# Opening by channel halves, the gate input mixed one stage later, and the middle stage's small vector work moved

## The reference

```
mod = silu(c) @ ada_w[0] + ada_b[0]            # shift sh1, scale sc1, four more parts
h   = x * (1 + sc1) + sh1                      # both per channel
xx  = previous token of h - h
xs  = h + xx * mu[m]       for m in r, k, v, w (decay), a, g (gate)
r, k, v = xs_r @ W_r, xs_k @ W_k, xs_v @ W_v   # 1024 x 1024 each
w = decay(tanh(xs_w @ w1) @ w2);  a = sigmoid(a0 + xs_a @ a1 @ a2)
g = sigmoid(xs_g @ g1) @ g2
bonus = sum over a head (r * k * r_k) * v      # added to the scan's normed output
y = recurrence over the tokens (S, w, k, v, a), then norm, bonus, * g, @ w_out
```

## Time and profile before

| what | value |
|---|---|
| three timed runs | 1457.09, 1460.92, 1460.15 us (median 1460.15) |
| the profiled execution's own time | 1451.71 us |
| its span, first to last instruction | 1449.9 us |
| TensorE busy in the span | 94% |
| VectorE, ScalarE, GpSimd busy | 63%, 46%, 15% |
| mean granted TensorE clock | 0.973 of full |

### The profile page before, as it was taken

One profiled execution on the slowest core, in us unless ns is written; L12 is line 12 of the kernel. 1 busy time (PEld: TensorE's weight loads), 2 busy tenths in 40 slices (PEclk: granted clock), 3 DMA queues, 4 the chain that ended last, 5 costly groups with the idle time before them and its releaser, 6 DMA issues. The chain is left out here.

```text
span 1449.9 us, 18487 instructions
## 1 busy us (share of the span) xinstructions
PE 1361.2 (94%) x7282; PEld 1118.8 (77%) x7282; DVE 907.5 (63%) x1245; ACT 671.2 (46%) x960; POOL 215.9 (15%) x123
## 2 busy tenths in 40 slices
PE   6999899889999989999999989989999989989998
PEld 2685568867888877677888868978887879978987
DVE  0775892668878757567765464665545677555564
ACT  1453333146444353646444326563472767426562
POOL 0001432104000022404000000300001332500210
PEclk8999999989999989999999999999999999999999
DMA  9751353055988864644876537834534441118940
GB/s 346 248 189 65 117 208 142 1 175 196 309 275 303 292 179 154 233 144 132 259 237 216 174 121 165 205 121 127 185 133 132 153 153 60 31 43 202 225 143 30
DMA packets 160360, 247.18 MB, mean 170 GB/s; under 512 B 15048, under 2 KB 100012, under 8 KB 159760
## 3 DMA queue, kind: packets, MB, share of 16 engines
q1 hardware_dynamic: 158944, 239.61, 52.4%
q0 software_dynamic: 1328, 6.38, 1.2%
HBM read 244.86 MB, written 4.24 MB: 172 GB/s over the span
## 5 line engine op out<-in xcount | busy, mean ns | idle before, releaser
L199 DVE TENSOR_TENSOR w_lo<-w_raw,w_hi 128x2048 fp32r<-128x2048 f32 (+3 forms) x176 | 403.3, 2298 | 247.4 <-ACT w_hi L190 247.2
L211 PE MATMUL ps<-w_hi,act_hi 128*128 128x512 f32 (+4 forms) x1216 | 472.3, 388 | 17.0 <-DVE act_lo L964 6.4
L212 PE MATMUL ps<-w_lo,act_hi 128*128 128x512 f32 (+4 forms) x1216 | 463.7, 381 | 0.0
L213 PE MATMUL ps<-w_hi,act_lo 128*128 128x512 f32 (+4 forms) x1216 | 463.4, 381 | 0.0
L190 ACT CAST w_hi<-w_raw 128x2048 fp32r<-128x2048 f32 (+3 forms) x176 | 316.7, 1806 | 255.4 <-PE ps L213 215.5
L211 PEld LDWEIGHTS ps<-w_hi,act_hi 128*128 128x128 f32 x1216 | 231.1, 190 | 63.9 <-issue 15.1
L213 PEld LDWEIGHTS ps<-w_hi,act_lo 128*128 128x128 f32 x1216 | 230.9, 190 | 36.8
L212 PEld LDWEIGHTS ps<-w_lo,act_hi 128*128 128x128 f32 x1216 | 231.2, 190 | 34.2 <-issue 0.7
L211 PE MATMUL ps<-w_hi,ffn_gh 128*128 128x512 f32 x176 | 69.7, 396 | 0.0
L771 POOL TENSOR_TENSOR nstat<-nstat,con 128x1 f32<-128x1 f32 x8 | 5.5, 682 | 424.9 <-DVE nstat L766 424.9
L213 PE MATMUL ps<-w_hi,ffn_gl 128*128 128x512 f32 x176 | 68.6, 390 | 0.0
(11 more groups left out here) (509 smaller groups left out, 1827.4 us busy)
## 6 DMA issues: line engine op xcount, KB each, us to landing
w_raw<-in_ffn_w_in SPq DMA_DIRECT2D x88, 512.0 KB, 5.0
w_raw<-in_fox_w_in SPq DMA_DIRECT2D x32, 912.0 KB, 8.2
w_raw<-in_ada_w SPq DMA_DIRECT2D x28, 1024.0 KB, 6.5
w_raw<-in_ffn_w_out SPq DMA_DIRECT2D x20, 1024.0 KB, 5.9
w_raw<-in_rwkv_w_rkv SPq DMA_DIRECT2D x12, 1024.0 KB, 5.9
con<-in_ada_w SPq DMA_DIRECT2D x48, 256.0 KB, 5.3
w_raw<-in_gla_w_in SPq DMA_DIRECT2D x10, 896.0 KB, 4.8
w_raw<-in_gdn_w_in SPq DMA_DIRECT2D x10, 896.0 KB, 4.8
```

The costliest lines, as they stand in the source:

```text
L199: self.nc.vector.tensor_tensor(lo[:, s, 0:c["nk"], 0:c["width"]], self.raw[:, c["slot"], 0:c["nk"], 0:c["width"]], hi[:, s, 0:c["nk"], 0:c ...
L211: nc.tensor.matmul(out(t)[:, 0:w], xh[:, k, tok], hi[:, s, j, 0:w], start=start, stop=False)
L212: nc.tensor.matmul(out(t)[:, 0:w], xh[:, k, tok], lo[:, s, j, 0:w], start=False, stop=False)
L213: return nc.tensor.matmul(out(t)[:, 0:w], xl[:, k, tok], hi[:, s, j, 0:w], start=False, stop=stop)
```

## The change

The diff touches the time mix's four stages, the helpers `dve_cols` and `mix`, and the order of the first four modulation items.

1. `stage_begin` and `stage_rwkv_in` become one stage, `stage_rwkv_open`. The items come in the order shift a, scale a, shift b, scale b (`first`), so that after two items the modulation of the first 512 channels is complete. x is loaded in two halves of 512 channels, after the fourth and after the eighth chunk. h, the difference, the mix and the first operand are computed for each half by itself. All of h is computed on ScalarE.
2. `keep_warm` has 3 matmuls in place of 12. The three low-rank weights are asked for after the third weight chunk behind the ring, and not before.
3. The mix of the gate input (8 instructions) moves from the end of this stage to the beginning of `stage_rwkv_low`, on VectorE, behind the memset; TensorE waits for it block by block at L1619.
4. In `stage_rwkv_mid` the product with r_k, its sums and the memsets are cut up and put behind the copies of units 4 to 7, 9 and 11 (`between`). GpSimd's bonus product waits for them.
5. There too `more` is called once ahead of TensorE's wait for the last copy, and from `u = 2` on, where it was called from `u = 4` on.

```diff
-    def dve_cols(self, dve, sem):
+    def dve_cols(self, dve, sem, n=0, end=None):
-def mix(core, dve, sem, m, dx, h, xs):
-    for k in range(KD):
+def mix(core, dve, sem, m, dx, h, xs, part=slice(0, KD)):
+    for k in range(part.start, part.stop):
...
@@ stage_rwkv_open, sync
+            core.issue(sp, opening[4]["g"])
+            tokens(0)
+            core.issue(sp, opening[-1]["g"] + 1)
+            tokens(1)
+            core.issue(sp, chunks[len(chunks) // 2]["g"])
             sp.dma_start(w1[:, :, :], ...
-            core.issue(sp, chunks[len(chunks) // 2]["g"])
@@ tensor
+            ada.pe_sums(pe, sem, 1)
+            ada.pe_turn(pe, sem, 0)
+            ada.pe_turn(pe, sem, 1)
+            tokens(0)
+            ada.pe_sums(pe, sem, 2)
+            ada.pe_sums(pe, sem, 3)
+            pe.wait_ge(sem("ada_cols"), 2)
+            ada.pe_turn(pe, sem, 2)
+            ada.pe_turn(pe, sem, 3)
+            tokens(1)
+            core.keep_warm(3, 3, core.x[:, 0, 0:COLS])
-            core.keep_warm(12, 3, core.x[:, 0, 0:COLS])
@@ scalar
+            ada.act_part(act, sem, 1)
+            tokens(0)
+            ada.act_part(act, sem, 2)
+            operand(0, 0)
+            ada.act_part(act, sem, 3)
+            core.split_hi(act, hi, chunks[0])
+            tokens(1)
+            core.split_hi(act, hi, chunks[1])
+            operand(0, 1)
@@ vector
+            def shifted(q):
+                dve.wait_ge(sem("h"), KG * q + KG)
+                nc.vector.tensor_scalar(dx[:, part[q], 0:1], ...
+                nc.vector.tensor_tensor(dx[:, part[q], 1:T], ...
+                dve.wait_ge(sem("diff"), 2 * q + 2)
+                mix(core, dve, sem, 0, dx, h, xs, part[q])
...
+            ada.dve_cols(dve, sem, 0, 2)
+            shifted(0)
+            operand(0, 0)
+            ada.dve_cols(dve, sem, 2, 4)
+            core.split_lo(dve, hi, lo, chunks[0])
+            shifted(1)
+            operand(0, 1)
...
@@ stage_rwkv_low, vector
             v.memset(low[64:65, 0:2, 0, :], 1.0).then_inc(sem("ones"), 1)
+            mix(core, dve, sem, 5, dx, h, gate_in)
@@ stage_rwkv_mid, tensor
             b_grams(len(units) - 1)
+            more(1)
             pe.wait_ge(sem("gram"), len(units))
...
                     kv(u - 1)
-                    if u > 2:
-                        more(1)
+                    more(1)
@@ vector
+            def between(u):
+                if u in (4, 5):
+                    v.tensor_tensor(rk[:, t, :], rk[:, t, :], rows[:, 2, :], ALU.mult)
+                if u in (6, 7):
+                    dve.wait_ge(sem("bonus"), t + 1)
+                    v.reduce_sum(w["bonus"][:, H64 * t:H64 * t + H64], ...
+                if u == 9:
+                    v.memset(inv[:, :, :], 0.0)
+                if u == 11:
+                    v.memset(inv ... [:, 0:1024:33], 1.0)
+                    v.memset(state[:, :, :], 0.0)
@@ program
-        first, later, last = mod[0:4], mod[4:10], mod[20:22] + mod[16:18]
+        first, later, last = [mod[0], mod[2], mod[1], mod[3]], mod[4:10], mod[20:22] + mod[16:18]
```

More of the change, by code:

```diff
@@ L342, in act_part @@
         core.nc.scalar.copy(self.part[n % self.depth][:, :], self.sums).then_inc(sem("ada_part"), 1)
-    def dve_cols(self, dve, sem):
+    def dve_cols(self, dve, sem, n=0, end=None):
         core, nb = self.core, COLS // P
+        end = len(self.items) if end is None else end
         one = lambda b: 0.0 if b // 2 in (SH1, SH2) else 1.0
-        dve.wait_ge(sem("ada_turn"), len(self.items))
-        n = 0
-        while n < len(self.items):
+        dve.wait_ge(sem("ada_turn"), end)
+        while n < end:
             l, b = self.items[n]
             m = n + 1
-            while m < len(self.items) and self.items[m] == (l, b + m - n) and one(b + m - n) == one(b):
+            while m < end and self.items[m] == (l, b + m - n) and one(b + m - n) == one(b):
                 m += 1
@@ L453, in column @@
     return core.modc[:, l, KD * part:KD * part + KD]
[L456 to L543, removed]
@@ L1453, in stage_rwkv_in @@
     k_k = core.gates
+    rows = core.place("rows", [P, 3, P], core.s0)
+    cs = core.place("csig", [P, KD], core.s0 + 2048)
+    crow = core.place("crow", [P, P], core.s0 + 2048 + 64)
+    ada = Ada(core, core.s0 + 4096, items, 0, 1)
+    scale, bias = column(core, 0, SC1), column(core, 0, SH1)
     flat = lambda x: x[:, :, :].rearrange("p i d -> p (i d)")
@@ L1456, in stage_rwkv_in @@
     decay_in, gate_in = m.a[:, :, :].rearrange("p i (k t) -> p (i k) t", t=T), m.g[:, :, :].rearrange("p i (k t) -> p (i k) t", t=T)
+    opening = [c for l, b in items for c in core.mod[l, b]]
     job = [blk for n in "rkv" for blk in core.jobs[f"rwkv_{n}"]]
@@ L1463, in stage_rwkv_in @@
     part = [slice(q * KG, q * KG + KG) for q in range(2)]
-    with core.stage("rwkv_in") as (block, sem):
+    with core.stage("rwkv_open") as (block, sem):
         def steps(split, taken, operand, mixed, after):
-            for n in range(len(chunks) + NSPL):
+            for n in range(1, len(chunks) + NSPL):
                 if n % per == 0 and n < len(chunks):
                     mixed(n // per)
-                    if n == 0:
-                        operand(0, 0)
-                        operand(0, 1)
                 if n > per and n < len(chunks) and n % per in (1, 2):
@@ L1508, in _, with tokens @@
         def _(act):
+            def tokens(q):
+                act.wait_ge(sem("ada_cols"), 2 * q + 2)
+                for k in range(4 * q, 4 * q + 4):
+                    act.wait_ge(sem("x_turned"), k // 2 + 1)
+                    nc.scalar.activation(h[:, k, :], ps[:, 4 + k // 2, k % 2 * T:k % 2 * T + T], ACT.Identity, scale=scale[:, k:k + 1],
+                                         bias=bias[:, k:k + 1]).then_inc(sem("h"), 1)
             def operand(i, q):
@@ L1553, in keys @@
                     nc.vector.tensor_scalar(st[:, 32:64], st[:, 0:32], 1e-24, None, ALU.max).then_inc(sem("kk"), 1)
+            nc.vector.memset(core.condz[:, :, :], 0.0).then_inc(sem("zero"), 1)
+            dve.wait_ge(sem("zero"), 1)
+            dve.wait_ge(sem("sig"), 1)
+            nc.vector.tensor_tensor(core.condz[:, :, 0], cs[:, :], ps[:, 3, 0:KD], ALU.mult).then_inc(sem("cond"), 1)
+            dve.wait_ge(sem("cols"), 3)
+            ada.dve_cols(dve, sem, 0, 2)
[5 more added lines that the diff above has]
+            operand(0, 1)
             steps(lambda c: core.split_lo(dve, hi, lo, c), lambda n: None, operand, mixed, keys)
@@ L1558, in _, with stage_rwkv_low @@
             mix(core, dve, sem, 5, dx, h, gate_in)
-def stage_rwkv_low(core, m, w, xs, low_w, key, at, free, later):
+def stage_rwkv_low(core, m, w, h, dx, xs, low_w, key, at, free, later):
     nc, a, ps = core.nc, core.a, core.ps
@@ L1760, in more @@
                         ada.pe_sums(pe, sem, done)
+                    if done == 1:
+                        pe.wait_ge(sem("across_e"), 1)
                     if 1 <= done <= len(items):
@@ L1998, in _ @@
                         nc.scalar.copy(dst, ps[:, i, :]).then_inc(sem("kv_out"), 1)
-                if u % 2 and u > 3:
+                if u % 2 and u > 1:
                     more(1)
@@ L2071, in _ @@
                                   ps[:, pair_bank(u):pair_bank(u) + 2, 0:T]).then_inc(sem("gram"), 1)
+                between(u)
             dve.wait_ge(sem("gram"), len(units))
@@ L2213, in rwkv @@
     w["rk"] = core.place("rk", [P, NT, D], w["rk_at"])
-    stage_rwkv_low(core, m, w, xs, low_w, key, core.s1, m.free, later[0])
+    stage_rwkv_low(core, m, w, h, dx, xs, low_w, key, core.s1, m.free, later[0])
     stage_rwkv_mid(core, m, w, later)
```

74 lines of the change are left out of this document (56 added, 18 removed).

## The result

The changed kernel took 1441.06 us (median of four executions, 1439.62 to 1444.98), the kernel before 1459.39: a ratio of 0.9866, interval 0.9831 to 0.9902; by the medians this is 18 us. The forecast was 1447, 13 us, with a lower end of 1440. The ratio puts the changed kernel at 1439.8 against the 1459.39, just outside. Two further comparisons, with six executions of the changed kernel each, gave 0.9915 (0.9887 to 0.9943) and 0.9891 (0.9847 to 0.9934); two with only two executions each gave 0.9828 (0.9673 to 0.9983) and 0.9852 (0.9698 to 1.0007). In all, 20 executions of the changed kernel lie between 1437 and 1449 (median 1442.2), 124 of the kernel before between 1451 and 1476 (median 1460.5): the change is worth 16 to 18 us, more than forecast, with one step of the forecast absent and another of the wrong sign.

A forecast was written before the change was run, and what follows sets the result against it. TensorE was taken as the bound, busy for 1361 of 1450 us. The terms -12.0 - 2.0 - 1.5 + 2.5 = -13.0 gave 1438.7 by the profiled execution, 1447.1 on the median: forecast 1447, range 1440 to 1455.

The forecast's parts named there:

- Part 1, the opening: Start of the time mix: computing by halves starts the r, k and v products earlier, 12.0 us saved, between 8 and 14.
- The chain named on ScalarE and VectorE: Opening: weight splits, activations, second half's difference and mix, and operand halves on these engines, ready for the second weight at 44.9.
- chunk 8's landing: Opening: the first weight chunk (counted from 0), asked for at 24.24 us, lands 8.6 later, at 32.8, as now.
- chunk 9's low part: Opening: VectorE's low part of the second weight chunk ends at 44.9 us; TensorE, done at 43.8, waits for it.
- Part 2, the gate mix: End of the projections' stage: without this VectorE work the next stage starts at 118.4 in place of 120.4, 2.0 us saved.
- 1.5 for the clock: Low-rank stage's start: after a gap of 1.4 us in place of 3.4 the clock may stay full; 1.5 us saved.
- Parts 3 and 4, the middle stage: Middle stage: cut-up vector work and moved modulation items together lose 2.5 us, bounds 0.9 gained to 6.4 lost.
- The gain behind `across`: Middle stage after the last copy: item gone (-1.85), DMA waits gone (-1.3), one more turn (+1.0).
- the 4.7 ahead of it: Middle stage: TensorE goes on from its wait for the last copy at 184.6 us in place of 179.86, 4.7 later.
- the third copy waits for TensorE as now: nothing is gained: Middle stage: removing VectorE work ahead of the first copy looks like up to 1.2 us gained, but gives nothing.
- Putting the sum on the median: Whole kernel: the saving made against the profiled 1451.7 us, 8.4 below the median, is carried over to give 1447.1.
- The range allowed for the middle stage's clock: Middle stage: a full clock from 182.4 to 190.7 us gives 3.4 back; a clock pulled down makes it 6.4 lost.

The follow-up runs named there:

- after_again: The changed kernel run once more, unchanged, against the kernel before: ratio 0.9915 (0.9887 to 0.9943).
- after_third: The changed kernel run a third time, unchanged, against the kernel before: ratio 0.9891 (0.9847 to 0.9934).
- mix_moved_alone: The kernel before with one edit, the gate input's mix moved to the beginning of the low-rank stage: ratio 0.9965 (0.9939 to 0.9990).
- before_t1: One more trace of the kernel before, unchanged: the time mix ends at 309.6 us, the rest takes 1159.8.
- once_no_between: The changed kernel with the gate input mixed once and VectorE's small middle-stage work back ahead of the first copy: ratio 0.9927 (0.9902 to 0.9952).
- tuned: The changed kernel with gate mix once, no warm-up, second weight chunk's low part ahead of the operand's low half: ratio 0.9902 (0.9870 to 0.9933).

## Why the prediction was wrong

- **Part 1, the opening: right in size, partly by luck.** Forecast: first product at 38.3, second chunk at 44.9, last projection at 105.0, 12.0 saved. Measured in the first pair: 39.4, 45.2, 105.2, 11.8; on the mean of all traces 11.4. The chain named on ScalarE and VectorE (chunk 8's landing, ScalarE's h, the second half's mix, chunk 9's low part) is the one in the trace: chunk 9 was ready at 44.2. But TensorE didn't wait for it there, it came to it at 45.2, because three terms of its own chain were off and nearly cancelled. The last modulation chunk was used at 28.16 and not 30.1; the turns of both last items came behind it, 3.58 us and not 1.87; the three warm-up matmuls took 4.7 us, where the forecast had 1.3 at the full clock and 2.6 at half, half of what the earlier trace rows give. TensorE waited for chunk 9, for 0.8 us, in after_again and after_third.
- **Part 2, the gate mix: failed.** The forecast took the mix out of the projections' stage (2.0 us) and, from the shorter gap, 1.5 for the clock. The change doesn't do that: it adds the second mix and leaves the first. Gap 3.45 as before, clock 0.56 in place of 0.68. I had read the context line of the diff as part of the move. mix_moved_alone shows that the 3.5 us would be there in its trace.
- **Parts 3 and 4, the middle stage: wrong sign.** Forecast: 2.5 us lost. Measured: 1.1 won in the first pair, 3.3 on the means. The gain behind `across` was right: 2.1 in the first pair (47.49 for 49.63; forecast 2.15). What failed is the 4.7 ahead of it, which came out as 1.0, and in it the sentence "the third copy waits for TensorE as now: nothing is gained". From the start of the fourth copy to that of the last the copies did take 3.2 longer (15.3 for 12.1; forecast 3.7), but they began as much earlier, so that the last copy was not late against the stage's start; only the item's 1.0 is left. The sentence rested on a trace whose clock was half from 158.6 to 165.4 us. Where the stage's first 8 us have the low clock it holds, as after_again's third copy shows, and the forecast's 4.7 is 4.1 there (26.7 for 22.6). In the other traces of before TensorE has the full clock there and stands waiting for the first copy, which the cut-up work takes away:

```profile
166.09 1.45 PE L1778 MATMUL ps<-turned 64*128 64x256 f32 x8 [2.46 <-DVE gram L2070]
```

- **Putting the sum on the median: a step without ground.** The profiled execution was 8.4 us under the median. I took the difference to be the same for both kernels. It isn't a constant: the changed kernel's profiled execution was 3.9 over its median. On the means of the traces, 5 of before's 8.4 us lie inside the time mix, where the change was at work. The range allowed for the middle stage's clock as this one trace had it, not for its falling for 23 us as in before_t1.

Summed on the means of the traces: 0.6 too much for Part 1, 3.4 too much for Part 2, 5.8 too little for the middle stage (2.5 lost against 3.3 won), 0.8 too little behind it. That makes 15.7 us in place of 13.0, and 1444.5, inside the range. The last 5 us to the 1439.8 of the result stand in no trace; the later comparisons put the changed kernel at 0.9915 and 0.9891 in place of 0.9866, so that part is most likely the draw of the first four executions, and the missed range is in part bad luck. Of the 3.3 in the middle stage, 2.7 hang on the one fall in before_t1: without it the middle stage took 72.6 before, 0.6 more than after, and the end of the time mix is 12.5 us apart.

## What to carry to other kernels

Before costing a moved instruction, find the line with a minus: a move whose source stands as context is an addition. A profile is one draw of the clock; a sum made on it can be carried to the median only for stages in which that draw was ordinary, so look in the table by stretches for where the clock was low or unusually high along the changed path, and work each wait out at both clocks: here the same edit cost 3.1 us at the one and saved 0.9 at the other. A block of matrix products without gaps passes a moved start on nearly one to one (12.0 us earlier gave 11.7, 22.7 later gave 22.8).

## What the runs showed of the hardware

- The granted clock in the same code differed from execution to execution: the low-rank stage took 35.1, 36.8, 37.9 or 40.6 us, `across` to `turn_up` 46 to 60, with the mean clock of an execution between 0.957 and 0.980 and 10 us for each 0.01 of it.
- Behind an idle time of TensorE of 3.45 us at the stage change the clock was low for a time in eleven of the fourteen traces that have it (the low-rank stage took 36.8 to 38.0 us), and stayed full in three (35.1); behind one of 1.4 it was full at first in all four traces that have it, and fell later in the stage in two of them (40.6).
- Once low, the clock stayed low for long while TensorE had work without a gap: at 0.50 for 30.7 us in once_no_between, busy for all of them, 23.8 in tuned and 20.5 in before_t1.
- The Trainium skill, "TensorE: Matmul & The Clock Gate", Part 1, says that the clock follows how busy TensorE was recently. The traces agree with it only in part. The clock fell behind idle times, though not each time, and in the stretches of the line above it stayed low while TensorE was busy throughout. Three warm-up matmuls or none made no difference to the time (0.9883 without, 0.9891 with them).
- The record of the granted clock says nothing of the time ahead of its first entry. after_again's gives 1.00 from 18 to 22 us, where sixteen turns took 3.58 us against 2.01, so the mean clocks above count the first 11 to 27 us as full.
